# Weaving the columns of weight blocks and moving two feed-forward parts' weights by 64 and 128 bytes

## The reference, cut to what matters

```python
def conv_ffn(h, w_up, conv_w, conv_b, w_down):          # blocks 0 and 1 ("f0", "f1")
    a, b = jnp.split(h @ w_up, 2, axis=-1)              # 1024 -> 2 * 2816
    ...                                                 # a causal convolution of a over 3 tokens
    return (jax.nn.silu(a) * b) @ w_down                # 2816 -> 1024

n2 = _rmsnorm(h, norm2_w)                               # block 2 ("f2")
ffn = (jax.nn.silu(n2 @ w_gate) * (n2 @ w_up)) @ w_down
```

## Time and profile before

| what | value |
|---|---|
| median of 3 runs | 898.44 us (898.28 to 898.51) |
| span of the profiled execution, first to last instruction | 896.5 us |
| TensorE clock granted | 1.000 of full speed |
| PE busy | 890.7 us, 99% of the span, 7875 matmuls |
| PEld busy | 864.5 us, 96% |
| DVE / ACT busy | 648.0 us (72%) / 491.7 us (55%) |
| DMA | 160.68 MB, 179 GB/s mean |

### The profile page before, as it was taken

How to read it: one execution, slowest core, us unless ns; L and a number is a source line. 1 busy time by engine, 2 the same in 40 slices (tenths; PEclk the granted TensorE clock), 3 DMA queues, 4 the chain that set the end, 5 groups by cost and what they waited for, 6 DMA issues and landing times.

```text
span 896.5 us, 18673 instructions
## 1 busy us (share of the span) xinstructions
PE 890.7 (99%) x7875; PEld 864.5 (96%) x7875; DVE 648.0 (72%) x1190; ACT 491.7 (55%) x843; POOL 44.0 (5%) x50
## 2 busy tenths in 40 slices
PE   8999999999999999999999999999999999999998
PEld 7999999999999998889999999999988999999998
DVE  6987657877767789785887777677678586565664
ACT  6763555564545567575565546457437464444451
POOL 2000001000000000000000001001132000000000
DMA  8743343565465544633555653654152255555541
GB/s 320 289 180 109 136 156 139 223 225 205 148 229 189 184 152 171 242 112 108 219 185 218 230 201 147 234 190 160 37 228 95 94 212 212 192 185 209 203 154 48
DMA packets 26002, 160.68 MB, mean 179 GB/s; under 512 B 3008, under 2 KB 4928, under 8 KB 7360
## 3 DMA queue, kind: packets, MB, share of 16 engines
q1 hardware_dynamic: 25344, 158.45, 48.5%
q10 hardware_dynamic: 576, 1.05, 0.4%
HBM read 158.18 MB, written 1.05 MB: 178 GB/s over the span
## 4 chain that ended last, share of the span: by engine, by line
PE 97%; DVE 1%; DMA 1%; SPq 0%; issue 0%; ACT 0%
PE ps L412 95%; PE ps L428 2%; DMA raw<-in_w 1%; DVE arena L1716 0%; DVE wl L1266 0%; DVE arena L1700 0%; SPq L2564 0%; DVE arena L1772 0%; DVE arena L1791 0%; DVE xt L1462 0%; DVE wl L1482 0%; DVE arena L1713 0%; ACT wh L2209 0%; DVE arena L1695 0%; DVE arena L1709 0%
## 5 line engine op out<-in xcount | busy, mean ns | idle before, releaser
L1266 DVE TENSOR_TENSOR wl<-raw,wh 128x1024 fp32r<-128x1024 f32 x280 | 329.3, 1224 | 124.6 <-ACT wh L2065 124.3
L412 PE MATMUL ps<-xh,wh 128*128 128x256 f32 (+1 forms) x1264 | 352.6, 279 | 0.4 <-DVE wl L1482 0.4
L412 PE MATMUL ps<-xl,wh 128*128 128x256 f32 (+1 forms) x1264 | 350.3, 277 | 0.0
L412 PE MATMUL ps<-xh,wl 128*128 128x256 f32 (+1 forms) x1264 | 350.3, 277 | 0.0
L2065 ACT CAST wh<-raw 128x1024 fp32r<-128x1024 f32 x280 | 277.0, 1048 | 118.5 <-PE ps L412 106.4
L412 PEld LDWEIGHTS ps<-xh,wh 128*128 128x128 f32 x1264 | 237.5, 188 | 2.3 <-issue 1.1
L412 PEld LDWEIGHTS ps<-xl,wh 128*128 128x128 f32 x1264 | 237.5, 188 | 0.1
L412 PEld LDWEIGHTS ps<-xh,wl 128*128 128x128 f32 x1264 | 237.5, 188 | 0.0
L412 PE MATMUL ps<-fl,wh 128*128 128x256 f32 x528 | 145.9, 276 | 0.0
L412 PE MATMUL ps<-fh,wl 128*128 128x256 f32 x528 | 145.9, 276 | 0.0
L412 PE MATMUL ps<-fh,wh 128*128 128x256 f32 x528 | 145.9, 276 | 0.0
(11 more groups left out here) (249 smaller groups left out, 1052.4 us busy)
## 6 DMA issues: line engine op xcount, KB each, us to landing
raw<-in_w SPq DMA_DIRECT2D x144, 1024.0 KB, 4.9
raw<-in_w ACTq DMA_DIRECT2D x4, 256.0 KB, 5.3
xt<-in_x SPq DMA_DIRECT2D x4, 256.0 KB, 6.8
raw<-in_w SPq DMA_DIRECT2D x4, 256.0 KB, 8.2
arena<-in_mem SPq DMA_DIRECT2D x1, 1024.0 KB, 8.5
out<-xt SPq DMA_DIRECT2D x8, 128.0 KB, 1.9
arena<-in_sel SPq DMA_DIRECT2D x3, 256.0 KB, 5.7
small<-in_small SPq DMA_DIRECT2D x1, 623.0 KB, 6.4
```

Source lines behind the costliest of these rows:

```text
L412: return pe.matmul(out, lhsT, rhs, start=start, stop=stop, skip_group_check=True)
L1266: v.tensor_tensor(L[:, s], src[:, s], f32(H[:, s]), ALU.subtract).then_inc(*w_lo.up(split(i, a)))
```

## The change

Where the weights are the stationary operand, the columns of a unit's two blocks now lie alternately. The host puts column k of block 0 at column 2k and column k of block 1 at 2k + 1 of their 256, and each product loads every second column (`slice(j, 256, 2)`). In the down units, pairs of blocks are woven in the same way. So each LDWEIGHTS reads 128 values that are 8 bytes apart over 1024 bytes, where it read 128 neighbours over 512 bytes. The nine units of `unit_t` (now named `PLAIN`) and the four that are read from `raw` keep their layout. Beside that, the units of f1 begin 16 columns (64 bytes) and those of f2 32 columns (128 bytes) later in their slots than before; those of f0 and of the projections stay where they were.

```diff
-WOFF = {U[n]: 32 for n in ("m0v0", "m0v1", "m1v0", "m1v1", "Av0", "Av1", "kvv", "Cv0", "Cv1")}
+PLAIN = ("m0v0", "m0v1", "m1v0", "m1v1", "Av0", "Av1", "kvv", "Cv0", "Cv1")
+WOFF = {U[n]: 32 for n in PLAIN}
+WOFF.update({U[n]: {"f1": 16, "f2": 32}[n[:2]] for n in NAMES if n[:2] in ("f1", "f2")})
 WOFF.update({U[n]: 48 for n in ("Ck0", "Ck1", "Cu0", "Cu1")})
...
                 for j in range(2):
-                    o = slice(j * 128, (j + 1) * 128)
+                    o = slice(j, 256, 2)
                     last = mm3(P[:, j * 256:j * 256 + T], H[:, c, o], L[:, c, o], x_h, x_l, c == 0 and j == 0, c == 7)
...
                     for o in range(8):
                         acc = banks[4 + o // 2][:, (o % 2) * 256:(o % 2) * 256 + 256]
-                        cs = slice(o * 128, (o + 1) * 128)
+                        cs = slice(o // 2 * 256 + o % 2, (o // 2 + 1) * 256, 2)
                         last = mm3(acc, H[:, j, cs], L[:, j, cs], fch(fh_, f), fch(fl_, f), f == 0 and o % 2 == 0, False)
...
-    d["w"] = np.stack([units[n] for n in unit_names()])
+    woven = lambda u: u.reshape(128, 8, 2, 128).transpose(0, 1, 3, 2).reshape(128, 2048)
+    d["w"] = np.stack([units[n] if n in WHOLE + PLAIN else woven(units[n]) for n in unit_names()])
```

## The result

| | before | changed |
|---|---|---|
| median of the runs | 898.48 us | 938.55 us |
| span of the profiled execution | 896.5 us | 936.7 us |
| ratio | 1 | 1.0446 (95% interval 1.0433 to 1.0458) |

The account below looks back on a forecast made before the run. It took PE's matmul count times step as the bound: 14.3 - 0.3 + 6.7 + 0 = +20.7 us on the 896.5 us span, 917.2 us, so 919 us as median. Range 890 to 952 us, the forecast's own 904 to 935 us.

Parts of the forecast that it names:

- rival 3: Woven loads meet the moving stream twice as often; disturbance 6.6 ns in f0 and projections, 15.6 in f1/f2; 947 us; chance 0.20.
- PE bounds the kernel and nothing off it matters: Whole kernel: time is matmul count times step; casts and transfers have slack, so their part is 0.
- The starts of f1 and f2: 3168 matmuls in f1 and f2 go to badly placed distances, 113.3 to 117.8 ns each: +14.3 us.
- The woven blocks: 3024 matmuls in f0 and the projections rise 2.2 ns, the middle between 113.3 and 117.8: +6.7 us.
- the rule of two hits: Weight loads: two values in each 16-byte SBUF line suffice for full rate, so a woven load is as fast as before.
- The floor of 110 ns: Lowest matmul step, estimated from the transposes' 110 ns as a load little disturbed by moving data.
- Rival 1: Woven matmuls: both streams cover 1024 bytes at equal pace and may never meet; step 110 ns, 876.8 us; chance 0.20.
- Rival 2: Neither starts nor weaving matters; 113.3 ns and the copies' 116.9 ns have other reasons than addresses; 898.4 us; chance 0.08.
- Rival 4: Woven weight loads, reading every second value, run at half speed, step 220 ns: +683 us, 1,581 us; chance 0.05.
- f0 between 113.3 and 117.8: Sign to check in the changed profile: the matmul step in f0 lies between these two levels, in ns.
- f1 and f2 near 117.8: Sign to check in the changed profile: the matmul step there is near 117.8 ns, mean matmul duration up about 4.5 ns.

Follow-up runs that it names:

- starts_only: Kernel before with plain blocks, but the weights of f1 beginning 64 bytes and those of f2 128 bytes later: 913.25 us, ratio 1.0165.
- woven_only: Changed kernel without the new starts: blocks woven, f1 and f2 starting where they did before: 936.95 us, ratio 1.043.
- moving_back_woven: Changed kernel with activations and accumulator columns addressed from the last to the first, same product: 923.45 us, ratio 1.0278.
- starts_fine: Kernel before with the weights of f0 beginning 16 bytes later, of f1 32 bytes later, of f2 16 bytes earlier: 922.71 us, ratio 1.027.
- copies_placed: Kernel before with the copies xkh and xkl moved so that their two chunks have the distance 64: 914.23 us, ratio 1.0177.
- load_plain: Kernel before, plain blocks, every matmul moving only its first 64 columns except the first into each accumulator region: 1519.43 us.

## Why the prediction was right in direction and wrong in its terms

The direction was right, and the measured 938.55 us lies within the stated range (890 to 952 us). But the kernel lost 40.1 us where 20.7 were forecast, and 938.55 us is outside the 904 to 935 us that the forecast's own mechanism allowed. The range reached so far only to take in rival 3, whose mechanism is false. That the time fell inside it was luck. Point by point:

- *PE bounds the kernel and nothing off it matters.* Right: PE's waits went from 2.8 to 3.1 us, and DVE and ACT stayed far from the bound.
- *The starts of f1 and f2: +14.3 us.* Right for plain blocks (starts_only: +14.8 us, steps of 118.7 and 117.8 ns against 117.8 forecast). In the changed kernel this term isn't there: the woven step of 120.0 ns is longer than both, and on it the starts add 1.6 us. One reading of the distances was off: of the 36 matmuls on the copies in f2, the 18 of chunk 0 go from 192 to 320 bytes, which is 64 modulo 256, the good distance and not another bad one. At 4.5 ns each that is under 0.1 us.
- *The woven blocks: +2.2 ns in f0 and the projections, taken from the middle of two levels.* This is the step that failed. I treated weaving as something that only changes how the streams meet, and took the load's own time as given, on the 110 ns of the transposes and the rule of two hits. The load itself became 6.0 ns longer (111.9 to 117.9), and f1 and f2 are woven as well, though the term gave them nothing: 6384 x 6.0 = 38.3 us, against 38.5 us measured for weaving alone. The agreement is closer than the mechanism: compared matmul by matmul in the traces of woven_only and before, the 4752 of the feed-forward parts take 31.1 us more (6.5 ns each), the 1440 others of 256 columns 8.5 us (5.9 ns) and the 192 wide ones 0.6 us (3.3 ns), and what is not woven 0.8 us less. In the changed kernel the same comparison gives +18.4 us for f0 and the projections, where the term had +6.7, and +22.3 us for f1 and f2, where only the starts' +14.0 stood. In f0 the step rose by 6.7 ns and not by 2.2, three times as much.
- *The floor of 110 ns.* 1.9 ns too low: the load of a product alone takes 111.9 ns, a transpose's step is shorter.
- *Rival 1 (equal pace, 110 ns).* False as to time: a woven load alone takes 117.9 ns. Whether streams of equal pace can avoid each other stays open; moving_back_woven, at 117.8 ns, saves 2.2 ns of a load that has lost 6, and more than one cause fits it.
- *Rival 2 (distances don't matter).* False, by starts_only and starts_fine. Its doubt about the copies' steps was fair, though: copies_placed shows that the step is no function of the distance alone.
- *Rival 3 (twice the meetings, 947 us).* Closest in time, wrong in mechanism: the moving stream adds 2.1 to 3.2 ns to a woven load, where 6.6 and 15.6 ns were expected.
- *Rival 4 (load at half speed).* Not for every second value, but true for every fourth, 233.3 ns.

My own tests for it named "f0 between 113.3 and 117.8" and "f1 and f2 near 117.8"; all were 120 to 121. That f0 came out as slow as f1 and f2, although its starts had not moved, was the first sign that the load itself had changed.

## What to carry to other kernels

Where every matmul needs new weights, as here with 128 columns loaded and 256 moving, the step is close to the time of the weight load: keep the 128 float32 values of a stationary block next to each other. Every second value cost 6 ns of 112, every third 57 more. Before placing buffers by their distances, measure the load alone (a moving operand of 64 columns, at the same granted clock); that shows how much such tuning can bring. And a step read in a long stretch may be one of two lasting levels, so a change elsewhere can lose the better one.

## What the runs showed of the hardware that I had not expected

- At one and the same set of addresses, steps of 113.3 and 117.8 ns both last for 60 us and more, and what ran before the stretch decides which, not its own code.
- A shift of the weights by 16 bytes changes the step of an unbroken stretch from 113.3 to 118.8 ns.
- At a granted clock of 0.50 a load step takes 213 ns, plain or woven; at the full clock 111.9 and 117.9 ns. So the load slows down with TensorE's clock, and the cost of weaving shows only at the full one.
- In load_plain, with 64 moving columns behind nearly every load, PE had no idle time from 200 to 580 us and ran there at a granted clock of 0.50; the mean of the run was 0.556.
